# A gather in three pieces in place of two, the last between the activation transposes and the down products

## What is computed

```
def expert_block(args):
    xb, e = args
    return (jax.nn.silu(xb @ w_g[e]) * (xb @ w_u[e])) @ w_d[e]
...
yb = lax.map(expert_block, (xin, blk_e)).reshape(P, D)
yb = yb * row_w[:, None].astype(yb.dtype)
out = jnp.zeros((N, D), hf.dtype).at[row_tok].add(yb, mode='drop')
```

## Time and profile before

| | us |
|---|---|
| median of 3 runs | 1436.32 (1435.99 to 1436.57) |
| profiled execution, its own time | 1432.04 |
| its span, first to last instruction | 1430.1 |
| PE busy | 1329.5 |
| PE weight loads busy | 578.0 |
| VectorE busy | 432.0 |
| mean granted clock of TensorE | 0.979 |

### The profile page before, as it was taken

How to read it: one execution, slowest core, us unless ns; L and a number is a source line. 1 busy time by engine, 2 the same in 40 slices (tenths; PEclk the granted TensorE clock), 3 DMA queues, 4 the chain that set the end, 5 groups by cost and what they waited for, 6 DMA issues and landing times.

```text
span 1430.1 us, 17476 instructions
## 1 busy us (share of the span) xinstructions
PE 1329.5 (93%) x5883; PEld 578.0 (40%) x5883; DVE 432.0 (30%) x843; ACT 209.6 (15%) x453; POOL 186.7 (13%) x244
## 2 busy tenths in 40 slices
PE   5999988999969999999999999999999999999991
PEld 3878766644443333333333333333333333333330
DVE  4799345332253122112212211221221122112114
ACT  3132324510110000000000000000000000000002
POOL 3355433000000000100100010010001000100100
PEclk9999999999979999999999999999999999999996
DMA  5331311207048999999999999999999999999954
GB/s 203 110 121 60 118 59 60 96 23 293 0 191 316 385 419 413 403 402 413 403 405 407 406 403 389 414 402 392 418 409 396 401 414 402 394 413 416 400 239 181
DMA packets 93090, 435.78 MB, mean 305 GB/s; under 512 B 13488, under 2 KB 13517, under 8 KB 60810
## 3 DMA queue, kind: packets, MB, share of 16 engines
q1 hardware_dynamic: 86896, 429.23, 75.6%
q0 software_dynamic: 5312, 5.28, 1.1%
q10 hardware_dynamic: 858, 0.95, 0.2%
HBM read 429.10 MB, written 18.36 MB: 313 GB/s over the span
## 4 chain that ended last, share of the span: by engine, by line
issue 79%; PE 14%; POOL 2%; DVE 2%; DMA 1%; POOLq 1%; ACT 0%; ACTq 0%; DVEq 0%
PE ps_proj L1193 10%; PE ps_proj L1234 2%; POOL sb_tick L578 1%; POOL sb_tick L589 1%; DVE sb_x L1142 1%; DMA sb_rb_sb<-in_rel_bias 1%; PE ps_scores L1248 1%; PE ps_proj L1216 0%; POOL expert_rows L579 0%; DVE sb_x L1152 0%; DVE sb_conv L932 0%; DMA sb_weights<-expert_rows 0%; POOL sb_weights_r L557 0%; PE ps_proj L1225 0%; POOLq L596 0%
## 5 line engine op out<-in xcount | busy, mean ns | idle before, releaser
L1405 PE MATMUL ps_proj<-sb_weights,sb_scratch 128*64 128x512 f32 x1984 | 446.9, 592 | 0.8 <-DVE sb_scratch L1107 0.8
L1426 PE MATMUL ps_scores<-sb_weights,sb_scratch 128*64 128x512 f32 x992 | 240.2, 605 | 29.3 <-ACT sb_scratch L767 29.3
L1405 PEld LDWEIGHTS ps_proj<-sb_weights,sb_scratch 128*64 128x64 f32 x1984 | 142.3, 137 | 283.2 <-issue 282.1
L1382 PE MATMUL ps_proj<-sb_hT,sb_scratch 128*64 128x512 f32 x1008 | 240.5, 599 | 0.0
L1117 DVE TENSOR_TENSOR sb_scratch<-sb_scratch,ps_proj 128x256 f32<-128x256 f32 x62 | 26.1, 421 | 589.2 <-ACT sb_scratch L765 589.2
L578 POOL TENSOR_TENSOR sb_tick<-sb_tick 1x1 f32<-1x1 f32 x62 | 11.7, 188 | 1042.7 <-ACT sb_scratch L773 1042.7
L1193 PE MATMUL ps_proj<-sb_hT_r,sb_weights_r 128*128 128x512 f32 x512 | 130.1, 408 | 2.9 <-POOL sb_weights_r L557 2.9
L1382 PEld LDWEIGHTS ps_proj<-sb_hT,sb_scratch 128*64 128x64 f32 x1008 | 73.0, 138 | 145.6 <-issue 145.6
L1193 PEld LDWEIGHTS ps_proj<-sb_hT_r,sb_weights_r 128*128 128x128 f32 x512 | 99.2, 197 | 31.7 <-issue 10.4
L1426 PEld LDWEIGHTS ps_scores<-sb_weights,sb_scratch 128*64 128x64 f32 x992 | 60.2, 136 | 125.3 <-issue 81.2
L765 ACT ACTIVATE sb_scratch<-ps_proj 128x256 f32<-128x256 f32 x62 | 23.8, 384 | 545.4 <-PE ps_proj L1405 545.4
(11 more groups left out here) (221 smaller groups left out, 800.7 us busy)
## 6 DMA issues: line engine op xcount, KB each, us to landing
sb_weights<-in_w_exp_down SPq DMA_DIRECT2D x124, 1024.0 KB, 9.4
sb_weights<-in_w_exp_gate SPq DMA_DIRECT2D x124, 1024.0 KB, 8.8
sb_weights<-in_w_exp_up SPq DMA_DIRECT2D x124, 1024.0 KB, 10.7
sb_weights<-in_w_in SPq DMA_DIRECT2D x9, 2048.0 KB, 7.9
sb_x<-in_x SPq DMA_DIRECT2D x8, 512.0 KB, 9.0
sb_weights<-in_w_out SPq DMA_DIRECT2D x2, 2048.0 KB, 10.6
sb_weights<-expert_rows SPq DMA_DIRECT2D x4, 1024.0 KB, 7.8
sb_weights<-in_w_conv_pw SPq DMA_DIRECT2D x1, 2048.0 KB, 7.7
```

What stands on the lines that cost most here:

```text
L1382: last = mm(ps_rows[g * BLK:(g + 1) * BLK, :], onehot[:, t, :], h2[:, t, g * NW:(g + 1) * NW], start=t == 0, stop=t == T - 1)
L1405: last = mm(ps_gu[g * BLK:(g + 1) * BLK, :].rearrange("p (a n) -> p a n", a=2), hTb[:, c, half * BLK:(half + 1) * BLK], weights[:, place(p ...
L1426: last = mm(ps_y[g * BLK:(g + 1) * BLK, :], actT[:, j, half * BLK:(half + 1) * BLK], weights[:, place(parity, 4 + half), 2 * j + g, :], st ...
```

## The change

`gather` is called three times in a block where it was called twice. Between the halves of the gate/up products stand tiles 0 and 1 in place of 0, 1 and 2; after the second half stands tile 2 in place of tile 3; tile 3 now stands behind the transposes of the activation, ahead of the wait for ScalarE's copy of them. The number of matmuls and their order within the gather stay.

```diff
                     if half == 0:
 
                         pe.wait_ge(hot_b, b + 2)
-                        gather(range(T - 1))
-                gather([T - 1])
+                        gather(range(T - 2))
+                gather([T - 2])
                 pe.wait_ge(act_ready, b + 1)
                 for c in range(2):
                     last = pe.transpose(ps_actT[:, c * P:(c + 1) * P], act[:, c * P:(c + 1) * P], ident)
                 last.then_inc(actT_done, 1)
-
+                gather([T - 1])
 
                 pe.wait_ge(actT_ready, b + 1)
```

## The result

| | before | changed |
|---|---|---|
| median, us | 1436.32 (4 runs, 1435.99 to 1436.57) | 1402.44 (4 runs, 1401.0 to 1403.4) |
| profiled execution, its own time | 1432.04 | 1401.0 |
| its span | 1430.1 | 1399.2 |

The ratio is 0.9771, 95% interval 0.9757 to 0.9785: faster by 2.3%, 33.9 us. The predicted time was 1401, the range 1396.5 to 1413.

What follows compares the result with a forecast made beforehand. PE was taken to set the pace, 15.69 us a block; -0.86 + 0.24 = -0.62 us times 62 blocks gives -38.4, plus 2.8 us of weight waits is -35.6: 1401 us, range 1396.5 to 1413.

Steps and rivals of the forecast that it cites:

- What bounds the kernel: Over the expert blocks, PE sets the pace at 15.69 us each and the weight loads follow it.
- Step 1: Between the gate/up halves, eight gather matmuls stand in place of twelve: 0.86 us less per block.
- Step 2: After the second half, one tile still fills the activation gap, which stays 1.10 us: change 0.
- Step 3: Behind the activation transposes, a gather tile covers ScalarE's copy: 1.15 us in place of 0.91, 0.24 more (0.15 to 0.39).
- What is late next: VectorE's copy of the gathered rows ends later, still 0.8 us before PE's row transposes want it: no wait.
- The weights: Loads need 15.34 us a block against PE's 15.07; the 16.0 us cushion runs out, PE waits 2.8 us late in the loop.
- the first rival: PE paces to the end of the loop, transfers reaching 15.3 us or less: 1397.9 us; chance 0.28.
- The rival with 15.53 us: Weights take over in mid-loop at a pace of 15.53 us: time 1411.4, or 1420.3 without reserve; chance 0.22.
- Slower: PE's waits for weights lower the clock, costing 3.15 us per gather group; 1460 us at twenty such blocks; chance 0.04.
- nothing gained: After the gather's move, some wait not shown in rows holds the down products back as much: 1436 us; chance 0.04.

Runs made afterwards that it cites:

- e1: Against the changed kernel: last gather tile moved from behind the transposes into the activation gap, now holding two; 1425.8 us, ratio 0.9942 to the kernel before.
- e2: Against the changed kernel: three gather tiles between the halves, none in the activation gap, one behind the transposes; 1454.84 us, ratio 1.0134 to the kernel before.
- e5: Against the kernel before: first load of each down pair issued about 2.9 us sooner, PE's order untouched; 1434.79 us, ratio 1.0001.
- e4: Against the changed kernel: one gather tile between the halves, two in the activation gap, one behind the transposes; 1400.3 us, ratio 0.9766 to the kernel before.
- e6: Against the changed kernel: gather of tiles 0 and 1 left out, so rows of half the tokens are missing; 1398.46 us, ratio 0.9749 to the kernel before.

## Why the prediction came out as it did

- **What bounds the kernel**: right. PE's order alone moved the time (e1 and e2 by their pace times 62 blocks), and earlier loads alone (e5) moved nothing.
- **Step 1**, -0.86: measured 2.57 - 1.71 = -0.86.
- **Step 2**, the gap stays: 1.11 us, and as long when empty (e2).
- **Step 3**, +0.24, measured +0.31: this is the term that was mis-sized. Two transposes take 0.37 us before a matmul of the gather can follow, not the 0.29 that I halved from four. The piece takes 0.91, not 0.86, but the down half behind it gets 0.06 back. It lay inside the bounds of 0.15 to 0.39. The pace is so 15.15 in place of 15.07, and 62 x 0.54 = 33.5 us, against 33.9 and 32.2 measured.
- **What is late next**: VectorE's copy has 0.9 us to spare; I had 0.8. The 0.4 us in that sum, by which the last matmul's record was to outlive its step, is not what its row gives: 1.03 - 0.86 = 0.17, and 1.08 - 0.91 is 0.17 here too. The transposes and the piece, 0.13 us longer than I had them, made up for part of it.
- **The weights**: the forecast had a pace of 15.34 us for them, and e4 shows 15.4 once they lead. What failed is its consequence, 2.8 us of waits in the last blocks. The forecast asked 3.7 + 15.1 = 18.8 us of a cushion of 16.0; measured are 16.0 - 0.6 = 15.4, which is about 62 x (15.4 - 15.15). PE, slower than I thought by 0.08 us a block, asked 5 us less, the stream, a little slower too, some of it back. PE paced to the end, as in the first rival, but not for that rival's reason (transfers at 15.3 us or less): the cushion just lasted for 62 blocks. The two errors, 4.9 us too much gain on PE and 2.8 us of waits that didn't come, nearly cancel. It is luck that 1401 is closer to 1402.4 than its parts were.
- **The rival with 15.53 us** fell: its cushion gives out in mid-loop and its time is 1411, and neither came. Its first source, a share of 1.01 that can't rise beyond 1.02, says little: 405 GB/s showed 1.01 and 415 shows 1.02, so the share rose by 1% where the bytes rose by more than 2%. Its second source was right and I used it wrongly. The 408.7 GB/s of the Trainium skill, "DMA: Bandwidth & Descriptors", section "iDMA fabric — 4 AXI ports for 8 engines, asymmetric across TPBs", are for a stream of loads alone, and I divided the scatters' bytes by them too. The loads of a block are 6.29 MB, so by that figure a block takes 15.39 us, an estimate. The trace agrees: the loads alone ran at 408 GB/s where they set the pace of e4, though two thirds of their bytes go in rows longer than the 4 KiB that the Trainium skill's figure is for. Over the loop of the changed kernel they ran at 342.70 MB / 832.95 us = 411 GB/s, from the same DMA view as the last slices above:

```profile
q1 hardware_dynamic: 61067, 342.70, 100.4%
```

- **Slower, and nothing gained**: neither came. No wait held the down products back, and the granted clock stayed at 1.00 in e6 through more waiting than the forecast had. The price of that rival, 3.15 us, took a row's full length (6.59) less a step (3.44); length against length it is 6.59 - 3.60 = 2.99.
- The median lies 4.3 us above the profiled execution before and 1.4 us after. The loop starts at 427.4 us in the one profile and at 429.9 in the other, ahead of anything that was changed; this is the spread of single executions, and the pace per block is the steadier measure: 15.14 to 15.15 us in both profiles of the changed kernel.

## What to carry to other kernels

When an engine waits for a short step of another (here 0.5 us for a copy), a piece of independent work of about that length is worth putting there, taken from a place where nothing was covered; what it costs there is about what it sticks out beyond the wait (by the rows 0.86 - 0.47 = 0.39 us, measured 0.31). Before counting such a gain over all iterations, read how far the loads are ahead and how fast they can go at best: cushion divided by the difference of the paces is the number of iterations for which the gain is real (16.0 / 0.41 = 39 in e4, and more than 62 in the changed kernel). Once it is spent (e4, e6), further work on the engine buys nothing.

## What the runs showed of the hardware that I had not expected

The same stream of 1 MiB loads is steadier with a longer queue: 372 to 418 GB/s in slices at a time to landing of 10.7 us, 412 to 419 at 15.2 us. The DMA share hardly tells the two apart (1.01 and 1.02). The loads alone reached 408 GB/s where they set the pace, and 411 over the loop of the changed kernel. And 97 waits of PE for a load, the longest 1.4 us, in the 53 blocks or so that e6 spent so, left the granted clock at 1.00 (2.4 GHz).
